# Compression chunks in pairs, in two buffers of their own, with a table that orders the loads

## The reference

```
h     = rms_norm(x, norm_w)
proj  = h @ w_in                       # 2048 x 7704 columns: 15 blocks of 512 and 24 gate columns
q_a, kc, vc, ks, vs, kw, vw, g, z_a, q_b, k_b, v_b, z_b = split(proj)
k_cmp = silu(blocks(rope(kc)) @ cmp_k_w1) @ cmp_k_w2     # w1: 4096 x 512
v_cmp = silu(blocks(vc) @ cmp_v_w1) @ cmp_v_w2
o_a   = gates * (compressed, selected and sliding window attention), 8 heads
o_b   = softmax map 0 - lambda * softmax map 1, 4 heads, per-head rms_norm
x     = x + concat(o_a * silu(z_a), o_b * silu(z_b)) @ w_out
out   = rms_norm(x, final_norm_w)
```

## Time and profile before

| | |
|---|---|
| median of 3 runs | 515.7 us (515.63 to 516.32) |
| the profiled execution | 515.5 us, its span 513.3 us |
| busy, share of the span | PE 97%, DVE 55%, ACT 44%, POOL 9% |
| mean granted PE clock | 0.996 of 2.4 GHz |
| DMA, mean over the span | 210 GB/s |
| chain that ended last | PE 93%, issue 2%, DMA 1%, DVE 1%, ACT 1% |

### The profile page before, as it was taken

The page is one execution under the profiler, slowest core; times in us unless marked ns, Lnnn a source line. Parts: engine busy times, 40 slices in busy tenths (PEclk is TensorE's granted clock), DMA queues, the critical chain, the costliest instruction groups (busy, mean ns, idle before and its releaser), DMA issues.

```text
span 513.3 us, 6145 instructions
## 1 busy us (share of the span) xinstructions
PE 500.3 (97%) x2454; PEld 406.0 (79%) x2454; DVE 282.6 (55%) x321; ACT 227.1 (44%) x311; POOL 45.2 (9%) x41
## 2 busy tenths in 40 slices
PE   7999999999999999999999999999999999999993
PEld 6788876667776788888888888888888878888882
DVE  3856813353443957676466647665545544644532
ACT  5847224233232644354644555464544353334231
POOL 1003300010010302010020000001000000113030
PEclk9999999999999999999999999999999999999998
DMA  8998449787778952444343444526864445455004
GB/s 275 412 420 303 163 165 343 282 313 290 305 282 312 348 213 98 165 155 147 109 140 111 160 163 153 185 83 222 332 266 165 170 177 202 189 174 222 14 1 163
DMA packets 17867, 107.69 MB, mean 210 GB/s; under 512 B 2224, under 2 KB 2736, under 8 KB 5936
## 3 DMA queue, kind: packets, MB, share of 16 engines
q1 hardware_dynamic: 16544, 104.86, 54.8%
q10 hardware_dynamic: 1296, 2.44, 1.4%
HBM read 105.20 MB, written 2.10 MB: 209 GB/s over the span
## 4 chain that ended last, share of the span: by engine, by line
PE 93%; issue 2%; DMA 1%; DVE 1%; SPq 1%; ACT 1%; POOLq 0%; POOL 0%; DVEq 0%
PE acc L962 25%; PE acc L964 24%; PE acc L963 24%; PE O L1002 3%; PE S L1104 3%; DMA raw<-stream 1%; PE S L1027 1%; PE S L1121 1%; PE acc L986 1%; PE acc L987 1%; PE acc L988 1%; PE S L1038 1%; PE S L1185 1%; PE S L964 1%; PE S L963 1%
## 5 line engine op out<-in xcount | busy, mean ns | idle before, releaser
L651 DVE TENSOR_TENSOR wlo<-raw,whi 128x2048 fp32r<-128x2048 f32 x72 | 166.4, 2313 | 184.6 <-ACT whi L388 184.4
L388 ACT ACTIVATE whi<-raw 128x2048 fp32r<-128x2048 f32 x72 | 138.1, 1918 | 171.5 <-PE acc L964 107.8
L962 PE MATMUL acc<-whi,hT_hi 128*128 128x512 f32 x432 | 172.6, 399 | 0.9 <-issue 0.9
L964 PE MATMUL acc<-whi,hT_lo 128*128 128x512 f32 x432 | 168.6, 390 | 0.0
L963 PE MATMUL acc<-wlo,hT_hi 128*128 128x512 f32 x432 | 168.3, 390 | 0.0
L962 PEld LDWEIGHTS acc<-whi,hT_hi 128*128 128x128 f32 x432 | 81.1, 188 | 29.4 <-issue 13.6
L964 PEld LDWEIGHTS acc<-whi,hT_lo 128*128 128x128 f32 x432 | 81.1, 188 | 17.4
L963 PEld LDWEIGHTS acc<-wlo,hT_hi 128*128 128x128 f32 x432 | 81.2, 188 | 15.8
L350 POOL TENSOR_TENSOR stage<-stage,stage 128x512 f32<-128x512 f32 (+1 forms) x16 | 25.0, 1574 | 193.1 <-DVE stage L694 193.1
L467 ACT ACTIVATE e<-S,small 128x128 f32<-128x128 f32 (+1 forms) x48 | 19.5, 419 | 26.1 <-DVE small L706 26.1
L962 PE MATMUL acc<-whi,mixA_hi 128*128 128x512 f32 x64 | 25.0, 391 | 0.0
(11 more groups left out here) (160 smaller groups left out, 491.2 us busy)
## 6 DMA issues: line engine op xcount, KB each, us to landing
raw<-stream SPq DMA_DIRECT2D x88, 1024.0 KB, 4.9
raw<-stream SPq DMA_DIRECT2D x6, 512.0 KB, 10.6
x_nat<-x_rows SPq DMA_DIRECT2D x2, 1024.0 KB, 13.1
x_nat<-x_rows SPq DMA_DIRECT2D x1, 2048.0 KB, 7.4
result<-x_nat SPq DMA_DIRECT2D x8, 256.0 KB, 3.2
xTs<-xT SPq DMA_DIRECT2D x3, 512.0 KB, 9.2
raw<-stream SPq DMA_DIRECT2D x4, 256.0 KB, 6.0
fw<-final_w ACTq DMA_DIRECT2D x1, 1024.0 KB, 5.3
```

Of the source, the lines that this page charges most:

```text
L388: act.activation(whi[:, n % SPLIT, :], raw[:, c % RAW, :], ACT.Copy).then_inc(hi_ready, 1)
L651: dve.tensor_tensor(wlo[:, n % SPLIT, :], raw[:, c % RAW, :], whi[:, n % SPLIT, :].bitcast(f32), ALU.subtract)\
L962: pe.matmul(acc_bank(n), xh, wh, start=k == 0, stop=False)
L964: last = pe.matmul(acc_bank(n), xl, wh, start=False, stop=k == KT - 1)
```

## The change

- The order in STREAM: compression chunks come in pairs, with two projection chunks between. The new order from 9 is in 9, ck 10, ck 11, in 12, in 13, ck 14, ck 15, in 16, in 17, ck 18, ck 19, and so on to cv 38, cv 39. Blocks 2, 3, 4 and 5 now end at 13, 21, 29 and 37; K_END and V_END stay 23 and 39. From chunk 40 on all is as before.
- Compression chunks get two buffers of their own, `row_raw` (16 KB in r1; `hid` moves within r1), with semaphores `row_in`. Projection chunks have the four `raw` buffers to themselves.
- SP issues in the order of a table LOADS: 4 to 8, 10, 11, 9, 12, 13, 16, 17, 20, 14, 15, 21, 24, 18, 19, 25, 28, 22, 23, 29, 32, 26, 27, 33, 36, 30, 31, 37, 40, 34, 35, 41, 42, 38, 39, 43 and then in order. The n-th projection chunk's load waits for the halves of the (n-4)-th; a compression chunk's load waits for PE's use of the one two before it.
- `cmp_keys` on PE moves from behind K_END + 3 to behind K_END + 2 (25).

```diff
 STREAM = _in[:9]
-for _i in range(16):
-
-    STREAM += ([_in[9 + _i]] if _i < 2 else [_in[8 + _i]] if _i > 2 else []) + [_cmp[_i]]
+for _i in range(0, 16, 2):
+
+    STREAM += _in[9 + max(_i - 1, 0):10 + _i] + _cmp[_i:_i + 2]
 STREAM += _in[24:]
...
+ROWS = [c for c, s in enumerate(STREAM) if s[0] in ("ck", "cv")]
+ROW_PLACE = {c: i for i, c in enumerate(ROWS)}
...
-RAW, SPLIT = 4, 3
+RAW, SPLIT, ROW_RAW = 4, 3, 2
+
+
+LOADS = HALVED[RAW:9] + ROWS[:ROW_RAW]
+for _i in range(0, len(ROWS), ROW_RAW):
+    _n = sum(c < ROWS[_i] for c in HALVED) + RAW + 1
+    LOADS += [c for c in HALVED[:_n] if c >= RAW and c not in LOADS] + ROWS[_i + ROW_RAW:_i + 2 * ROW_RAW]
+LOADS += [c for c in HALVED[RAW:] if c not in LOADS]
...
-        hid = sb("hid", [P, CMP_HIDDEN], at=r1)
+        hid = sb("hid", [P, CMP_HIDDEN], at=r1 + 28672)
+        row_raw = sb("row_raw", [P, ROW_RAW, CH * NB], at=r1)
...
-            for c in range(RAW, N_CHUNKS):
-                before = c - RAW
-                if before in PLACE:
-                    sp.wait_ge(hi_ready, PLACE[before] + 1)
-                    sp.wait_ge(lo_ready, PLACE[before] + 1)
-                else:
-                    wait_used(sp, before)
+            for c in LOADS:
+                if c in ROW_PLACE:
+                    m = ROW_PLACE[c]
+                    if m >= ROW_RAW:
+                        wait_used(sp, ROWS[m - ROW_RAW])
+                    sp.dma_start(row_raw[:, m % ROW_RAW, :], stream[c, :, :]).then_inc(row_in[m % ROW_RAW], 16)
+                    continue
+                n = PLACE[c]
+                sp.wait_ge(hi_ready, n - RAW + 1)
+                sp.wait_ge(lo_ready, n - RAW + 1)
...
-                sp.dma_start(raw[:, c % RAW, :], stream[c, :, :]).then_inc(raw_in[c % RAW], 16)
+                sp.dma_start(raw[:, n % RAW, :], stream[c, :, :]).then_inc(raw_in[n % RAW], 16)
...
                 n = PLACE[c]
-                act.wait_ge(raw_in[c % RAW], 16 * (c // RAW))
+                act.wait_ge(raw_in[n % RAW], 16 * (n // RAW))
...
-                pe.wait_ge(raw_in[c % RAW], 16 * (c // RAW))
+                m = ROW_PLACE[c]
+                pe.wait_ge(row_in[m % ROW_RAW], 16 * (m // ROW_RAW + 1))
...
-                                     raw[:, c % RAW, i * NB:(i + 1) * NB], start=j == 0, stop=j == CMP_BLOCK // CH - 1,
+                                     row_raw[:, m % ROW_RAW, i * NB:(i + 1) * NB], start=j == 0, stop=j == CMP_BLOCK // CH - 1,
...
-                if c == K_END + 3:
+                if c == K_END + 2:
                     cmp_keys()
```

More of the change, by code:

```diff
@@ L210, in program @@
         raw_in = [sem(f"raw_in{i}") for i in range(RAW)]
+        row_in = [sem(f"row_in{i}") for i in range(ROW_RAW)]
         hi_ready, lo_ready = sem("hi_ready"), sem("lo_ready")
@@ L385, in split_hi @@
                 n = PLACE[c]
-                act.wait_ge(raw_in[c % RAW], 16 * (c // RAW))
+                act.wait_ge(raw_in[n % RAW], 16 * (n // RAW))
                 wait_used(act, HALVED[n - SPLIT])
-                act.activation(whi[:, n % SPLIT, :], raw[:, c % RAW, :], ACT.Copy).then_inc(hi_ready, 1)
+                act.activation(whi[:, n % SPLIT, :], raw[:, n % RAW, :], ACT.Copy).then_inc(hi_ready, 1)
             def split_hi_piece(i):
@@ L650, in split_lo @@
                 dve.wait_ge(hi_ready, n + 1)
-                dve.tensor_tensor(wlo[:, n % SPLIT, :], raw[:, c % RAW, :], whi[:, n % SPLIT, :].bitcast(f32), ALU.subtract)\
+                dve.tensor_tensor(wlo[:, n % SPLIT, :], raw[:, n % RAW, :], whi[:, n % SPLIT, :].bitcast(f32), ALU.subtract)\
                     .then_inc(lo_ready, 1)
```

## The result

The changed kernel takes 523.41 us (median of 4, 522.47 to 524.16) against 515.87 us (median of 4, 515.63 to 516.32): ratio 1.0145, 95% interval 1.0133 to 1.0157. A second set of runs gave 523.99 us (522.70 to 524.32) against 515.87 us, ratio 1.0150 (1.0136 to 1.0164). The forecast was 521.2 us, slower, with 519.5 to 524.4 as its range.

The account below looks back on a forecast made before the run. PE, busy 97% of the span, bounds the kernel, so its waits are lost: 515.5 + 4.65 + 2.85 - 1.0 - 0.95 = 521.05 us, 521.2 with the runs' median 0.2 higher. Range 519.5 to 524.4 us.

Parts of the forecast that it names:

- What bounds the kernel: Whole span: PE is busy 97%, so every microsecond it is made to wait after the change is lost.
- Part 1: Behind rope blocks (ends 21, 29, 37), PE resumes at x+4.09, x being last product matmul's start; loss 4.65 us.
- Part 2: Behind the value block (end 13), PE resumes at x+5.39, x being its last product matmul's start; loss 2.85 us.
- Part 4: Chunk 16's late load, from waiting for a shared buffer, comes early with own buffers: gain 0.95 us.
- Part 3: Pairs 10-11, 18-19, 26-27, 34-35, without a take: each saves 0.25 us of switching, gain 1.0 us (0 to 1.2).
- What should cost nothing: Chunk 9's later load, SP's load queue, moved cmp_keys and chunk 28's half all have margin: no loss.
- rival (c): PE's clock falls once in the new idle stretches, for one projection chunk: + 5.45 us, 526.6 us; chance 0.03.
- The prediction's own case: Whole kernel: new waits outweigh savings, 520.2 to 523.0 us; chance 0.82.
- rival (b): Chunk 19's load lands late in each of four rounds, up to 0.8 us each: + 3.2, 524.4 us; chance 0.08.
- the clock below 1.00 inside the stage: Sign against the prediction: PE's clock falling in the compression stage, where it took no fall.
- (a): DVE finishes the low half behind each pair in time, leaving only savings of 2.95 us: 512.8 us; chance 0.05.
- (d): Whole kernel: savings and waits cancel to within 0.2%, with two of the four waits absent; chance 0.02.

Follow-up runs that it names:

- Experiments 1 to 3: Changed kernel with the splits behind the pairs made ahead of the takes: ropes only 516.10 us, value block only 518.73 us, both 512.29 us.
- order alone: New stream order, with cmp_keys moved, but buffers, semaphores and loads of the kernel before: 524.07 us, ratio 1.0153 against the kernel before.
- version 3: Changed kernel with chunks 16, 24, 32 and 40 split early, ahead of the takes: 512.29 us, ratio 0.9933 against the kernel before.
- experiments 1 to 4: Changed kernel with early splits for ropes (516.10 us), value block (518.73 us) or both (512.29 us), or with small matmuls filling the waits (521.00 us).
- buffers alone: Old alternating order with the new buffers and a load order made for it: 514.75 us, ratio 0.9975 against the kernel before.
- version 3's repeat: The changed kernel with both early split moves, run again: 512.50 us over 6 runs, ratio 0.9933 against the kernel before.
- the filled version: Changed kernel with 50 small matmuls before chunk 16 and 28 before 24, 32 and 40: 521.00 us, ratio 1.0103 against the kernel before.
- experiment 7: New order and early splits, but the shared buffers and loads of the kernel before: 516.19 us, ratio 1.0003 against the kernel before.
- experiment 1: Changed kernel with only the low halves of chunks 24, 32 and 40 split ahead of the ropes: 516.10 us, ratio 1.0009 against the kernel before.

## Why the prediction was right or wrong

**What bounds the kernel, and the new order.** Right. Each microsecond of waiting came through to the end, and the four waits stand where take and split said, and nowhere else. Experiments 1 to 3 show the cause by moving the split alone: each kind of wait goes with its own move, and order alone shows all four without buffers or table.

**Part 1, ropes.** x + 4.08 measured, x + 4.09 forecast. **Part 2, values.** x + 5.33 against x + 5.39. **Part 4, the old wait.** Gone, and worth 1.1 us by itself, 0.95 forecast.

**Part 3, the free pairs.** 0.34 us each rather than 0.25, above the bound of 0.29: the gap between the two chunks' starts is 0.89 us, the two passes and nothing more, and the way out was a little cheaper. But only three savings came, not four. The prediction counted four pairs without a wait and overlooked that the kernel before had 12 and 13 side by side already, with the gate transposes between, which now stand alone. The sum, 1.0 us, came out right by two errors that cancel. That seven pairs and not eight count fits version 3 and all of the experiments 1 to 4; that the gate transposes are the reason is read from the traces, and no run moved them. The rule of the Trainium skill (TensorEngine Tiling (Array Packing), Key Properties) that a change of mode drains TensorE and a change of tile doesn't agrees with the pairs' rows.

**What should cost nothing.** The loads' queue and chunk 9's load were as forecast: the changed kernel's list of waits has none on a load in the stage, where ACT had 54.1 us. cmp_keys and chunk 28's half made no wait.

**The step that failed** is in rival (c): "I take no fall", and its chance of 0.03. I had compared the new idle stretches (1.8 and 3.1 us) with the one at the kernel's end, where PE's clock stayed up for 4.2 us without work (from 504.7 to about 509.0). That was one execution. Over the eleven traces of this case the clock stays up between 2.4 and 5.2 us behind the last matmul (2.4 us in the traces of buffers alone and of version 3's repeat), so this stretch doesn't cover the wait of 3.1 us. For those of 1.8 us it would have, but they lie between two stretches of work, and in the three traces with such a fall the clock fell 1.1 to 1.4 us after PE was back. Judged by times and mean clocks it fell in all eight executions of the changed kernel, once or twice. Its price was too high in turn, 5.45 us for a whole chunk, where a fall costs 1.56 us. With one fall taken from the executions at 522.5 to 522.8 us and two from those at 523.9 to 524.3, 521 us are left, and the filled version, 521.0 us, is the forecast's sum without a fall. The Trainium skill's warning that waits between bursts throttle the clock (TensorE: Matmul & The Clock Gate, HAM oscillation) was borne out here and should have had a far larger chance; that waits of 1.8 us are enough is from these runs.

**The range.** The mechanism of the waits was right, but that the time lies in the range is in part luck. The prediction's own case ended at 523.0 us, and both medians, 523.4 and 524.0, are above it. What reaches 524.4 is rival (b), late loads, which didn't happen. And the clock below 1.00 inside the stage, which the prediction names as a sign that it is wrong, came.

**Rivals (a), (b), (d).** (a) didn't happen in this kernel, but its number, 512.8 us, is what the early splits gave, 512.3. (b) didn't happen; loads become a limit only with shared buffers and without the waits (experiment 7).

What makes 1.8 us enough for a fall is open. The pair of narrow matmuls ahead of it may count less as work than product matmuls do, but this isn't shown: no run had idle time of that length between full product matmuls, and behind the pair 18-19 of experiment 7 even 2.0 us led to no fall. Why the same program falls once in one execution and twice in another is open too. Nor is the kernel before wholly free of it by its times: one of its 17 executions in experiment 7 took 518.61 us with a mean clock of 0.991, and has no trace.

## What to carry to other kernels

When chunks that need preparation and chunks that don't share a stream, grouping the latter shortens the time that the helpers have for the next prepared chunk: look at what stands ahead of that preparation in the helpers' fixed programs, above all anything that waits for the bounding engine's last result. Moving that preparation ahead of the wait turned 1.5% slower into 0.7% faster here, with the buffers of their own; with shared buffers it only came back to the old time. And price a new wait on TensorE with its clock, about 1.6 us for each fall, not by its length alone.

## What the runs showed of the hardware

The clock fell to 1.2 GHz behind idle stretches of 1.84 us, ahead of which PE had done sixteen narrow matmuls in 1.9 us; in the changed kernel's two profiles and in that of order alone this was 1.1 to 1.4 us after PE had come back to work at chunk 24. Behind a stretch of 3.1 us it fell just as PE came back, in the second profile of the changed kernel and in that of experiment 1, and not at all in the first. The five falls in the traces lasted 3.4 us each, and one cost about 1.6 us. By times and mean clocks, falls came in two of four executions where only 1.8 us stretches were left, and in five of ten where only the 3.1 us one was. At the kernel's end, with no work left, the clock stayed up between 2.4 and 5.2 us, differently in each execution, so the one stretch of a single trace says little about how much idle time the clock bears. Work that nothing needs, 28 to 50 small matmuls put into the wait, kept it up and made the kernel 2.1 to 2.7 us faster, each measured from the kernel before beside it, with all waits in place. Two compression chunks (128x32 tiles) in a row cost 2.06 us, two single ones 2.40.
